# First transfers and first TensorE work of a two-layer streaming encoder, in another order

## The reference

```
h = RMSNorm(x)
[uA|vA|q|k|v|cin|gB|gC|gates] = h @ w_in
A = gelu(uA) * (W_s(mask) . RMSNorm(gelu(vA)) + b_s)
B = softmax(q k^T / sqrt(dh) + relbias) v
C = gB * causal_dwconv3(gC * cin)
x = x + W_out( sum_b sigmoid(gates_b) * (branch_b @ W_branch_b) )
x = x + FFN(RMSNorm(x))     layer 0 dense SwiGLU, layer 1 top-2-of-8 experts
```

## Time and profile before

| | |
|---|---|
| median of 3 runs | 1873.61 us (1873.16 to 1874.46) |
| profiled execution, its own time | 1871.49 us |
| its span | 1869.6 us |
| PE busy | 1792.5 us, 96% |
| DVE busy | 1423.5 us, 76% |
| ACT busy | 1093.4 us, 58% |
| POOL busy | 35.5 us, 2% |
| moved by DMA | 487.08 MB, mean 261 GB/s |
| granted TensorE clock, mean of the span | 0.981 |

### The profile page before, as it was taken

How to read it: one execution, slowest core, us unless ns; L and a number is a source line. 1 busy time by engine, 2 the same in 40 slices (tenths; PEclk the granted TensorE clock), 3 DMA queues, 4 the chain that set the end, 5 groups by cost and what they waited for, 6 DMA issues and landing times.

```text
span 1869.6 us, 27425 instructions
## 1 busy us (share of the span) xinstructions
PE 1792.5 (96%) x10460; PEld 1598.2 (85%) x10460; DVE 1423.5 (76%) x1535; ACT 1093.4 (58%) x1055; POOL 35.5 (2%) x64
## 2 busy tenths in 40 slices
PE   7999999999999899969999999999999999999995
PEld 7988999999998899958888888888878888888884
DVE  6575667777765755657889798898888897988984
ACT  4353445333345344436777776777767767777773
POOL 1201000000000000000000000000000000000000
PEclk9998999999999999979999999999999999999998
DMA  9744544554444435266999999999989999999990
GB/s 348 253 141 149 178 158 158 159 180 158 162 155 140 135 104 168 91 225 234 378 368 347 326 367 330 383 360 338 346 318 387 367 357 321 365 350 370 356 366 26
DMA packets 253026, 487.08 MB, mean 261 GB/s; under 512 B 8000, under 2 KB 97120, under 8 KB 252640
## 3 DMA queue, kind: packets, MB, share of 16 engines
q1 hardware_dynamic: 247504, 466.64, 71.0%
q0 software_dynamic: 4336, 17.46, 2.7%
q10 hardware_dynamic: 1056, 1.18, 0.2%
HBM read 477.38 MB, written 7.88 MB: 260 GB/s over the span
## 4 chain that ended last, share of the span: by engine, by line
issue 66%; PE 28%; DVE 2%; ACT 2%; DMA 0%; POOL 0%; ACTq 0%; POOLq 0%
PE psum L1750 9%; PE psum L1752 8%; PE psum L1751 8%; ACT attn L855 1%; DVE w_lo L1061 1%; PE psum L1726 0%; PE psum L1725 0%; PE psum L1724 0%; DMA vec<-in_vecs 0%; PE psum L1620 0%; ACT w_hi L769 0%; PE psum L1669 0%; PE psum L1680 0%; DVE attn L1167 0%; ACT h_hi L779 0%
## 5 line engine op out<-in xcount | busy, mean ns | idle before, releaser
L1359 DVE TENSOR_TENSOR e_lo<-ring,e_hi 128x2048 fp32r<-128x2048 f32 x224 | 511.9, 2291 | 88.7 <-ACT e_hi L950 88.1
L950 ACT ACTIVATE e_hi<-ring 128x2048 fp32r<-128x2048 f32 x224 | 429.1, 1918 | 182.1 <-PE psum L1878 92.1
L1061 DVE TENSOR_TENSOR w_lo<-ring,w_hi 128x1024 fp32r<-128x1024 f32 x218 | 266.4, 1228 | 169.8 <-ACT w_hi L769 168.0
L1750 PE MATMUL psum<-h_hi,w_hi 128*128 128x288 f32 x1248 | 373.8, 300 | 18.8 <-DVE w_lo L1061 16.9
L1751 PE MATMUL psum<-h_lo,w_hi 128*128 128x288 f32 x1248 | 370.7, 297 | 0.0
L1752 PE MATMUL psum<-h_hi,w_lo 128*128 128x288 f32 x1248 | 369.4, 296 | 0.0
L769 ACT ACTIVATE w_hi<-ring 128x1024 fp32r<-128x1024 f32 x218 | 230.3, 1058 | 217.7 <-PE psum L1752 200.7
L1876 PE MATMUL psum<-e_hi,he_hi 128*128 128x512 f32 x896 | 356.2, 398 | 0.2 <-ACT he_lo L956 0.2
L1878 PE MATMUL psum<-e_hi,he_lo 128*128 128x512 f32 x896 | 351.9, 393 | 0.0
L1877 PE MATMUL psum<-e_lo,he_hi 128*128 128x512 f32 x896 | 351.4, 392 | 0.0
L1359 DVE TENSOR_TENSOR e_lo<-spare,e_hi 128x2048 fp32r<-128x2048 f32 x112 | 256.3, 2289 | 44.1 <-ACT e_hi L950 44.0
(11 more groups left out here) (287 smaller groups left out, 1985.6 us busy)
## 6 DMA issues: line engine op xcount, KB each, us to landing
ring<-in_e_w SPq DMA_DIRECT2D x224, 1024.0 KB, 5.8
spare<-in_e_w SPq DMA_DIRECT2D x112, 1024.0 KB, 5.6
ring<-in_w_in SPq DMA_DIRECT2D x56, 1024.0 KB, 5.2
ring<-in_w SPq DMA_DIRECT2D x33, 1024.0 KB, 5.2
ring<-in_w_branch SPq DMA_DIRECT2D x12, 1024.0 KB, 5.0
ring<-in_w_out SPq DMA_DIRECT2D x8, 1024.0 KB, 5.1
bias_ext<-attn POOLq DMA_DIRECT2D x2, 2048.0 KB, 9.7
bias<-bias_ext POOLq DMA_DIRECT2D x2, 1536.0 KB, 13.2
```

The source lines that it names most:

```text
L950: nc.scalar.activation(e_hi[c % BUFS][:, :], expert_ring[s][:, 0:PIECE_W], ACT.Copy).then_inc(piece_rounded, 1)
L1061: nc.vector.tensor_tensor(low, src, high.bitcast(f32), ALU.subtract).then_inc(split, 1)
L1359: nc.vector.tensor_tensor(e_lo[buf][:, :], expert_ring[s][:, 0:PIECE_W], e_hi[buf][:, :].bitcast(f32), ALU.subtract).then_inc(piece_split, 1)
L1750: nc.tensor.matmul(bank(name), high, src[0][:, k, :], start=(k == 0), stop=False)
```

## The change

x comes in four transfers of two tiles each, with a semaphore each. `vec` is issued by SP ahead of the weights instead of by POOL. ACT waits only for `eps`, and then does one activation on a 128x1 constant before x is needed. Its order, and DVE's, is now tiles 0 to 5, chunk 0, tiles 6 and 7, chunk 1, chunk 2, the squares, chunk 3. In layer 0 PE does three chunks before the mean of squares instead of two; layer 1 keeps its order. DVE sets `eps` and `mean_w` first, then zeroes bank 7 of PSUM, then banks 0 to 6. PE does 14 plain float32 matmuls of 128 columns, `mean_w` by `mean_w`, into bank 7, whose result is not used, before it waits for the rest. POOL waits until the third weight slot has landed, then does the bias rows of layer 0, the bias tiles, the inputs of layer 0, and the bias rows of layer 1, waiting for each store. DVE waits for both stores before it masks the bias, since the scores are written over `ext`.

```diff
@@ -55,6 +55,7 @@
 BIAS_W = 384
+WARM = 14
 EXT = 512
@@ -152,7 +153,8 @@
-    g = [("v", l, 0), ("v", l, 1), ("norm", 2 * l), ("v", l, 2), ("v", l, 3)]
+    early = 2 if l else 3
+    g = [("v", l, j) for j in range(early)] + [("norm", 2 * l)] + [("v", l, j) for j in range(early, BT)]
     g += [("q", l, 0), ("q", l, 1)] + [("vt", l, n) for n in range(3)] + [("q", l, 2), ("q", l, 3)]
@@ -263,6 +265,7 @@
         eps = sb("eps", [P, 1])
+        first_act = sb("first_act", [P, 1])
         vec = sb("vec", [P, VECS])
@@ -394,7 +397,7 @@
         bank_full = sem("bank_full")
-        x_in = [sem("x_in0"), sem("x_in1")]
+        x_in = [sem(f"x_in{i}") for i in range(4)]
         vec_in = sem("vec_in")
@@ -582,6 +585,7 @@
+            sp.dma_start(vec[:, :], vecs).then_inc(vec_in, 16)
             mixer(0)
@@ -690,21 +694,19 @@
-            def bias_rows():
-
-                for l in range(2):
-                    if l:
-                        pool.wait_ge(ext_stored, 16 * l)
-                    pool.dma_start(ext[:, :, EXT // 2 - 1:EXT - 1],
-                                   bias_rev[l:l + 1, :, 0:TAB - 1].broadcast_to([P, HEADS, TAB - 1]),
-                                   ).then_inc(ext_loaded, 16)
-                    pool.wait_ge(ext_loaded, 16 * (l + 1))
-                    nc.gpsimd.tensor_copy(ext[:, :, 0:EXT // 2 - 1], ext[:, :, EXT // 2 - 1:EXT // 2].broadcast_to(
-                        [P, HEADS, EXT // 2 - 1])).then_inc(ext_ready, 1)
-                    pool.wait_ge(ext_ready, 2 * l + 1)
-                    nc.gpsimd.memset(ext[:, :, EXT - 1:EXT], 0.0).then_inc(ext_ready, 1)
-                    pool.wait_ge(ext_ready, 2 * l + 2)
-                    pool.dma_start(bias_ext[l], ext.rearrange("p h c -> p (h c)")).then_inc(ext_stored, 16)
+            def bias_rows(l):
+
+                pool.dma_start(ext[:, :, EXT // 2 - 1:EXT - 1],
+                               bias_rev[l:l + 1, :, 0:TAB - 1].broadcast_to([P, HEADS, TAB - 1]),
+                               ).then_inc(ext_loaded, 16)
+                pool.wait_ge(ext_loaded, 16 * (l + 1))
+                nc.gpsimd.tensor_copy(ext[:, :, 0:EXT // 2 - 1], ext[:, :, EXT // 2 - 1:EXT // 2].broadcast_to(
+                    [P, HEADS, EXT // 2 - 1])).then_inc(ext_ready, 1)
+                pool.wait_ge(ext_ready, 2 * l + 1)
+                nc.gpsimd.memset(ext[:, :, EXT - 1:EXT], 0.0).then_inc(ext_ready, 1)
+                pool.wait_ge(ext_ready, 2 * l + 2)
+                pool.dma_start(bias_ext[l], ext.rearrange("p h c -> p (h c)")).then_inc(ext_stored, 16)
+                pool.wait_ge(ext_stored, 16 * (l + 1))
@@ -719,11 +721,11 @@
-            pool.dma_start(vec[:, :], vecs).then_inc(vec_in, 16)
-            bias_rows()
-            pool.wait_ge(ext_stored, 32)
+            pool.wait_ge(slot_loaded[2], 16)
+            bias_rows(0)
+            bias_tiles(0)
             layer_inputs(0)
-            bias_tiles(0)
+            bias_rows(1)
             pool.dma_start(rw[:, :, :], router.rearrange("(k p) e -> p k e", p=P)).then_inc(layer_in[5], 16)
@@ -754,9 +756,10 @@
             x_dram = x_t.rearrange("(k p) t -> p k t", p=P)
-            for k in range(2):
-                act.dma_start(x[:, 4 * k:4 * k + 4, :], x_dram[:, 4 * k:4 * k + 4, :]).then_inc(x_in[k], 16)
-            act.wait_ge(zeroed, 3)
+            for k in range(4):
+                act.dma_start(x[:, 2 * k:2 * k + 2, :], x_dram[:, 2 * k:2 * k + 2, :]).then_inc(x_in[k], 16)
+            act.wait_ge(zeroed, 1)
+            nc.scalar.activation(first_act[:, :], eps[:, :], ACT.Copy)
@@ -771,7 +774,7 @@
                 if n == 0:
-                    act.wait_ge(x_in[k // 4], 16)
+                    act.wait_ge(x_in[k // 2], 16)
                     act.wait_ge(vec_in, 16)
@@ -816,11 +819,11 @@
                         x_high(n, k)
-                        if k % 4 == 3:
-                            round_lead(first + k // 4)
+                        if k in (5, 7):
+                            round_lead(first + (k - 5) // 2)
+                    round_lead(first + 2)
                     for k in range(DT):
                         square(n, k)
-                    round_lead(first + 2)
                 round_lead(first + 3)
@@ -936,7 +939,7 @@
             act.wait_ge(state_stored, 64)
-            act.wait_ge(zeroed, 4)
+            act.wait_ge(zeroed, 5)
             for hf in range(2):
@@ -1122,9 +1125,10 @@
-            nc.vector.memset(psum[:, :, :], 0.0).then_inc(zeroed, 1)
             nc.vector.memset(eps[:, :], EPS).then_inc(zeroed, 1)
             nc.vector.memset(mean_w[:, :], 1.0 / D).then_inc(zeroed, 1)
+            nc.vector.memset(psum[:, 7, :], 0.0).then_inc(zeroed, 1)
+            nc.vector.memset(psum[:, 0:7, :], 0.0).then_inc(zeroed, 1)
             done(nc.vector.memset(valid[:, :], 1.0))
@@ -1138,10 +1142,12 @@
                     x_low(n, k)
-                    if l == 0 and k % 4 == 3:
-                        low_lead(first + k // 4)
+                    if l == 0 and k in (5, 7):
+                        low_lead(first + (k - 5) // 2)
+                if l == 0:
+                    low_lead(first + 2)
                 sum_squares(n)
-                for c in range(3 if l else 2, CHUNKS + 2):
+                for c in range(3, CHUNKS + 2):
                     low_lead(first + c)
@@ -1156,6 +1162,7 @@
                 dve.wait_ge(bias_loaded, 16 * (l + 1))
+                dve.wait_ge(ext_stored, 32)
                 nc.vector.memset(bias[0:CHUNK, :, 256 + CHUNK:BIAS_W], MASKED).then_inc(bias_masked, 1)
@@ -1753,11 +1760,15 @@
             pe.wait_ge(zeroed, 3)
+            for _ in range(WARM):
+                nc.tensor.matmul(psum[:, 7, 0:P], mean_w[:, :], mean_w[:, :], start=True, stop=True)
+            pe.wait_ge(zeroed, 4)
             pe.wait_ge(made, 5)
             for l in range(2):
-                features("v", l, range(2))
+                early = 2 if l else 3
+                features("v", l, range(early))
                 mean_sum(NORM_OF_LAYER[l])
-                features("v", l, range(2, BT))
+                features("v", l, range(early, BT))
                 features("q", l, range(2))
```

## The result

The changed kernel takes 1883.83 us (median of 5 runs, 1879.92 to 1885.53), the kernel before on the same chip 1873.16 us (5 runs, 1869.68 to 1874.46). The ratio is 1.006 with an interval of [1.0047, 1.0072]: slower by 0.5 to 0.7%, outside the predicted range. The profiled execution took 1879.92 us, the quickest of the five; its span is 1878.2 us, 8.6 us above that of before.

A forecast was written before the change was run, and what follows sets the result against it. PE, busy 96% of the span, was taken to bound the kernel. Terms of -1.2, -0.34 and -0.8 us summed to -2.3 us, taking the median from 1873.61 to 1871.3 us; range 1868.9 to 1874.0 us.

The forecast's parts named there:

- (c): 14 constant matmuls on PE at the start: delay nothing, clock lost again before data, shorter low-clock stretch, -0.8 us.
- the one on the slower side: Rival: DVE waits at the bias mask for the late second bias-row store; upper bound +0.9 us, 1874.5 us; chance 0.07.
- (a): Start of PE: table load and norm-vector wait go, first matmul at 12.1 instead of 13.28, -1.2 us.
- (b): PE's wait before chunk 2 goes, as chunk 2 is put ahead of the squares: -0.34 us.
- clock kept: Rival: PE's clock stays high over the pause before the first data; -4.2 us, 1869.4 us; chance 0.23.
- (d): PSUM memset split on DVE, first activation and extra x issues on ACT at the start: hidden, no cost.
- (e): POOL's bias rows wait for the third slot; second store lands at 76, before DVE's mask at 82.5: cost 0.

The follow-up runs named there:

- e1: The changed kernel with its 14 constant matmuls taken out: 1870.12 us, ratio 0.9985 to the kernel before.
- e10: The changed kernel without constant matmuls and without the early activation on the 128x1 constant: 1871.87 us in one profiled execution, the kernel before 1872.97 us.
- e9: The changed kernel without constant matmuls and with POOL's bias rows first as before: 1873.39 us in one profiled execution, the kernel before 1872.97 us.
- e4: The changed kernel with 10 constant matmuls instead of 14: 1879.66 us, ratio 1.0038 to the kernel before.
- e8: The changed kernel with 42 constant matmuls instead of 14: 1871.81 us, ratio 0.9988 to the kernel before.
- e2: The changed kernel with 18 constant matmuls instead of 14: 1871.5 us, ratio 0.9991 to the kernel before.
- e6: The changed kernel with 16 constant matmuls instead of 14: 1871.9 us, ratio 0.999 to the kernel before.
- e5: The changed kernel with 15 constant matmuls instead of 14: 1885.54 us, ratio 1.0062 to the kernel before.

## Why the prediction was wrong

**The step that failed** is (c), "They delay nothing: PE has no data before 12.1", together with "From 19 us on PE is back to back, so the terms are carried to the attention part, whose order is unchanged, and from there to the end." The constants were costed as time on PE's timeline and not as code in its list. Their 56 instructions moved the head of a loop that is reached 880 us later, and PE stops at each of two jumps: 12.8 us in the trace, 13.7 us between the medians of after and e1 (1883.83 - 1870.12, not measured side by side). A row that could have warned me lay in the trace of before: ACT, in the same loop, waited 5.20 us for "issue" ahead of `e_hi` at 1139.20. I read no wait beyond 811 us, since the diff didn't reach there. No rival held this; the one on the slower side had another mechanism and ended at +0.9 us.

**(a) Start of PE, right.** Predicted 12.1 and -1.2 us; 12.46 and -0.82, within its bounds. The third quarter of x came at 9.03 where I had 8.7; the rest of the sum (0.9, then 2.5) measured 0.86 and 2.57. That the table load had to go was wrong in its reason: e10 keeps it behind x's arrival, and its first matmul comes no later. That x needs POOL's queue out of the way was right, and larger than thought: e9.

**(b) The wait of 0.34 us, right.** It is gone.

**(c) The clock, right in its outcome, the constants mis-sized.** They started at 1.74, not 2.6, and took 4.96/14 = 0.35 us each, not 0.47, so they ended at 6.70, ahead of my 8 to 9.2, and the pause was 5.76 us where I allowed 2.9 to 4.6. The clock was lost over it. The low stretch shrank from 24 matmuls to 12, a gain of 5.89 - 4.54 = 1.35 us where I had 0.8. It is not the constants' doing: e1, with none, has 12 matmuls at 0.24 us too and needs 4.59 us for the 24, and e4, with ten, has 22 and needs 5.67. The length differs from trace to trace, with and without constants, so this part of the gain is luck. The rival "clock kept" needs constants up to the data; e8 has them, and it comes out where the forecast is.

**(d) and (e), right.** The second store landed at 70.4 where I had 76, 12 us ahead of the mask; ACT waited for no weights.

**The sum without the failed step** agrees with what was measured, but the measurement is coarse: e1 is the change but for the constants, and stands at -3.2 us ([0.9973, 0.9998] of the kernel before, -5 to -0.4 us) where the sum was -2.3; e2, e6 and e8, which have constants and no stop behind the head, stand at -1.7 to -1.8. That the mask came 2.34 us sooner, just the sum, is in part luck: (a) gave 0.4 less than forecast and the low stretch 0.55 more, and in e4, e5, e6 and e10 the mask came only 0.5 to 1.1 us sooner. Nor is the lead carried on exactly: from the mask to the first transposes went 772.5 us in after and e1, 774.1 in the kernel before and 775.1 to 776.3 in e2, e5, e6, e8 and e10. I did not look for the cause. e1 beats the changed kernel clearly and the kernel before just beyond noise, and nothing with constants is measurably better than it.

## What to carry to other kernels

Count what an edit adds to an engine's instruction list ahead of a runtime loop, not only its time: here 56 instructions that ran for 5 us in an idle stretch cost 13 us at two jumps, and 8 more or 56 fewer cost nothing. After such an edit look at the head of every loop for a wait with no releaser, and, if there is one, try the head a few instructions further on: here four (15 or 16 constants) were worth 13.6 us. Test the parts of a change one by one: here POOL's bias rows had to be moved out of x's way for the start to come sooner at all, and neither the early activation nor the warm-up brought anything measurable. What `vec` on SP, the four pieces of x and the new order of chunk 2 earn was not taken apart.

## What was not expected of the hardware

- PE's code comes in packets of 16384 bytes, one for some 256 instructions, through the DMA engines that the weights use. After a jump back, the block behind the head's was there some 5 us (4.9 to 5.4) after the head was passed with the engines full of weights (98% on q1), and 2.35 us with them half empty (1147.10 - 1144.75, 51%). At the entry without a jump there was no wait at the same instruction (889.20).
- A stop of 4.3 to 5.1 us costs more than itself: the granted clock fell to 0.52, the level of 1.2 GHz, and the eight intervals after the sixth matmul took 1.3 us more; at the second jump it was eleven and 2.2 us.
- The clock can fall after PE has started again. With 18 constants, which ended 4.51 us before the data, the first matmuls are at 0.13 us and only from 13.19 on at 0.24:

```profile
12.89 0.29 PE L1758 MATMUL psum<-h_lo,w_hi 128*128 128x288 f32 x1
13.02 0.37 PE L1759 MATMUL psum<-h_hi,w_lo 128*128 128x288 f32 x1
13.19 0.44 PE L1757 MATMUL psum<-h_hi,w_hi 128*128 128x288 f32 x1
13.43 0.44 PE L1758 MATMUL psum<-h_lo,w_hi 128*128 128x288 f32 x1
```
